# The pooling branch's product in the merge stage: one product of plain float32 tiles, or three passes over high and low parts

## The reference

```python
y_a = o @ w_branch_gla[l]
pooled = multiscale_pool(u)
y_b = jnp.einsum('blgc,gcd->blgd', pooled, w_pool_group[l]).reshape(bsz, length, D_MODEL)
y_b = (y_b * pool_scale[l]).astype(x.dtype)
merged = jax.nn.sigmoid(g_a) * y_a + jax.nn.sigmoid(g_b) * y_b
x = x + merged @ w_out[l]
```

## Time and profile before

| | us |
|---|---|
| median of 3 runs | 2587.4 (2586.15 to 2589.64) |
| profiled execution | 2586.93 |
| its span | 2585.1 |
| PE busy | 2535.0 (98%) |
| VectorE busy | 1857.0 (72%) |
| POOL busy | 1213.2 (47%) |
| ScalarE busy | 1039.5 (40%) |

### The profile page before, as it was taken

The page is one execution under the profiler, slowest core; times in us unless marked ns, Lnnn a source line. Parts: engine busy times, 40 slices in busy tenths (PEclk is TensorE's granted clock), DMA queues, the critical chain, the costliest instruction groups (busy, mean ns, idle before and its releaser), DMA issues. The chain is left out here.

```text
span 2585.1 us, 32147 instructions
## 1 busy us (share of the span) xinstructions
PE 2535.0 (98%) x12094; PEld 2051.7 (79%) x12094; DVE 1857.0 (72%) x2076; ACT 1039.5 (40%) x1463; POOL 1213.2 (47%) x764
## 2 busy tenths in 40 slices
PE   8999999999999999999999999999999999999998
PEld 6888788887787888887887778776886788878887
DVE  8756756558559666668879657666658767787988
ACT  6322444442124333234435212766455333444443
POOL 3322222224448888885333344241135888833332
PEclk9999999999999999999999999999999999999999
DMA  6433333345522343246642443402333676775544
GB/s 207 124 102 123 120 129 109 102 142 163 179 92 79 99 123 106 78 139 204 228 129 71 142 154 104 135 33 73 115 90 118 223 235 202 246 246 171 180 137 165
DMA packets 341055, 362.95 MB, mean 140 GB/s; under 512 B 21115, under 2 KB 256278, under 8 KB 340902
## 3 DMA queue, kind: packets, MB, share of 16 engines
q1 hardware_dynamic: 335686, 341.49, 41.5%
q10 hardware_dynamic: 5216, 19.40, 1.9%
HBM read 247.81 MB, written 111.99 MB: 139 GB/s over the span
## 5 line engine op out<-in xcount | busy, mean ns | idle before, releaser
L4024 PE MATMUL ps<-op_hi,sw_hi 128*128 128x512 f32 x1765 | 692.1, 392 | 10.4 <-POOL sw_lo L3920 3.1
L4024 PE MATMUL ps<-op_hi,sw_lo 128*128 128x512 f32 x1765 | 686.9, 389 | 0.0
L4024 PE MATMUL ps<-op_lo,sw_hi 128*128 128x512 f32 x1765 | 686.8, 389 | 0.0
L4024 PEld LDWEIGHTS ps<-op_hi,sw_hi 128*128 128x128 f32 x1765 | 331.3, 188 | 89.0 <-POOL sw_lo L3920 6.5
L4024 PEld LDWEIGHTS ps<-op_lo,sw_hi 128*128 128x128 f32 x1765 | 331.4, 188 | 69.4 <-issue 1.4
L4024 PEld LDWEIGHTS ps<-op_hi,sw_lo 128*128 128x128 f32 x1765 | 331.3, 188 | 69.4
L546 POOL TENSOR_TENSOR w_hi_t<-w_raw,ones 128x1024 fp32r<-128x1024 f32 (+1 forms) x54 | 99.5, 1848 | 462.6 <-DMA w_raw<-in_w_in 196.3
L3910 ACT ACTIVATE sw_hi<-sw_sumNone 128x512 fp32r<-128x512 f32 (+1 forms) x252 | 156.7, 623 | 312.8 <-PE ps L4024 205.4
L3920 POOL TENSOR_TENSOR sw_lo<-sw_sumNone,sw_hi 128x512 fp32r<-128x512 f32 x138 | 220.4, 1606 | 23.4 <-ACT sw_hi L3910 23.3
L3871 POOL TENSOR_TENSOR sw_sumNone<-sw_raw 128x512 f32<-128x512 f32 (+1 forms) x63 | 112.5, 1786 | 218.5 <-DVE sw_lo L3920 197.7
L3920 POOL TENSOR_TENSOR sw_lo<-sw_raw,sw_hi 128x512 fp32r<-128x512 f32 x109 | 156.9, 1446 | 65.4 <-ACT sw_hi L3910 65.3
(11 more groups left out here) (525 smaller groups left out, 5324.4 us busy)
## 6 DMA issues: line engine op xcount, KB each, us to landing
w_raw<-in_w_in SPq DMA_DIRECT2D x45, 512.0 KB, 4.6
sw_raw<-in_w_ffn_in SPq DMA_DIRECT2D x44, 512.0 KB, 5.4
sw_raw<-in_w_up SPq DMA_DIRECT2D x32, 512.0 KB, 7.0
hidden<-hidden_rows SPq DMA_DIRECT2D x16, 1024.0 KB, 5.0
sw_raw<-hidden SPq DMA_DIRECT2D x32, 512.0 KB, 5.4
op_raw<-down_differences SPq DMA_DIRECT2D x16, 1024.0 KB, 6.0
proj<-acc SPq DMA_DIRECT2D x56, 256.0 KB, 2.2
acc<-proj SPq DMA_DIRECT2D x28, 512.0 KB, 4.3
```

The lines of the kernel that those rows point to most:

```text
L4024: mm = pe.matmul(out, w, x[:, k, :], start=(k == 0 and i == 0 and r < 4), stop=(k == n - 1 and i == 2), skip_group_check=r >= 4)
```

## The change

The pooling branch's product is computed like the large ones. New tiles `pooled_hi`, `pooled_lo`, `wpool_hi` and `wpool_lo`, each 128x1024, hold the parts. ScalarE copies the weights into `wpool_hi` once, ahead of the first gates, and for each group the pooled rows into `pooled_hi`: the first behind gates(0), the others in rounds 1, 3 and 5 behind the gates of the next round. POOL subtracts once, `wpool_lo`, between units 1 and 2 of its sixteen. VectorE subtracts once for each group, `pooled_lo`: right behind `pool(0)`, and behind `split_lo` in rounds 1, 3 and 5. `yb(j)` is three passes of two matmuls. `pooled_ready` counts to 3 for each group instead of 1, and `wpool_loaded` to 18 instead of 16. The scan reads its ones from a column of the constant tile `ones` with step 0, where before a tile of ones was written by a memset.

```diff
--- before.py
+++ after.py
@@ -298,7 +298,7 @@
 LATER_PAIRED = {"sw_landed": ("gab_loaded", (128, 128)), "hid_stored": ("o_back", (80, 16)),
                 "x3_back": ("half_ready", (8, 8)), "x3_spilled": ("x1_spilled", (64, 64))}
 OPERANDS = (("r_loaded", 64), ("v_loaded", 64), ("qk_loaded", 128), ("o_stored", 96), ("u_loaded", 64),
-            ("gla_loaded", 128), ("wpool_loaded", 16))
+            ("gla_loaded", 128), ("wpool_loaded", 18))
 ODD_HEADS = (("merged_hi", 8), ("merged_lo", 8))
 X1_BACK = (("sc_fwd", 4), ("sc_tile", 4), ("vt_ready", 8), ("o_ready", 8))
 
@@ -1804,7 +1804,29 @@
 
         ub, csb, pooled = acc[:, 0, :], acc[:, 1:3, :].rearrange("p a t -> p (a t)"), acc[:, 3, :]
         gab = [(acc[:, 4, :], acc[:, 6, :]), (acc[:, 5, :], acc[:, 7, :])]
-        ones_row = ssq
+        ones_row = ones[:, 0:1].to_broadcast([P, T])
+        pooled_hi, pooled_lo = at("pooled_hi", [P, T], 68, F32R), at("pooled_lo", [P, T], 12, F32R)
+        wpool_hi, wpool_lo = at("wpool_hi", [P, T], 64, F32R), at("wpool_lo", [P, T], R0 + 128, F32R)
+        wpool_row = wpool[:, :, :].rearrange("p g c -> p (g c)")
+
+        def wpool_high(act):
+            act.wait_ge(S["wpool_loaded"], 16)
+            act.activation(wpool_hi[:, :], wpool_row, ACT.Copy).then_inc(S["wpool_loaded"], 1)
+
+        def wpool_low(pool):
+            pool.wait_ge(S["wpool_loaded"], 17)
+            pool.tensor_tensor(wpool_lo[:, :], wpool_row, wpool_hi[:, :].bitcast(F32), ALU.subtract)\
+                .then_inc(S["wpool_loaded"], 1)
+
+        def pooled_high(act, g):
+            act.wait_ge(S["pooled_ready"], 3 * g + 1)
+            act.activation(pooled_hi[:, :], pooled, ACT.Copy).then_inc(S["pooled_ready"], 1)
+
+        def pooled_low(dve, g):
+            dve.wait_ge(S["pooled_ready"], 3 * g + 2)
+            dve.tensor_tensor(pooled_lo[:, :], pooled, pooled_hi[:, :].bitcast(F32), ALU.subtract)\
+               .then_inc(S["pooled_ready"], 1)
+
         Z0 = 8
 
         def ya_wo_unit(sp, j):
@@ -1823,7 +1845,7 @@
                 if j:
                     sp.wait_ge(S["o_lo"], KT)
                 if j % 2 == 0 and g:
-                    sp.wait_ge(S["pooled_ready"], g)
+                    sp.wait_ge(S["pooled_ready"], 3 * g - 2)
                     sp.dma_start(ub, proj[(25 + g) * P:(26 + g) * P, :]).then_inc(S["u_loaded"], 16)
                 if j == 0:
                     sp.wait_ge(S["o_lo"], 5)
@@ -1853,18 +1875,18 @@
                         wait_k=(lambda k: pe.wait_ge(S["o_lo"], O_ORDER.index(k) + 1)) if j == 0 else None)
 
             def yb(j):
-                pe.wait_ge(S["wpool_loaded"], 16)
-                pe.wait_ge(S["pooled_ready"], j // 2 + 1)
+                pe.wait_ge(S["wpool_loaded"], 18)
+                pe.wait_ge(S["pooled_ready"], 3 * (j // 2) + 3)
                 if j == 0:
                     pe.wait_ge(S["o_rstd"], GH)
                 if j == 1:
                     pe.wait_ge(S["o_gate"], 4 * GH - 1)
                 if j >= 2:
                     pe.wait_ge(S["yb_scaled"], j - 1)
-                for b in range(2):
-                    mm = pe.matmul(yb_bank(j)[:, b * HALF:(b + 1) * HALF],
-                                   wpool[:, j // 2, j % 2 * P:(j % 2 + 1) * P],
-                                   pooled[:, b * HALF:(b + 1) * HALF], start=True, stop=True)
+                for n, (w, x) in enumerate(((wpool_hi, pooled_hi), (wpool_hi, pooled_lo), (wpool_lo, pooled_hi))):
+                    for b in range(2):
+                        mm = pe.matmul(yb_bank(j)[:, b * HALF:(b + 1) * HALF], w[:, j * P:(j + 1) * P],
+                                       x[:, b * HALF:(b + 1) * HALF], start=n == 0, stop=n == 2)
                 mm.then_inc(S["yb_ready"], 1)
 
             ya(0)
@@ -1884,10 +1906,14 @@
                 for g in gab[j % 2]:
                     act.activation(g, g, ACT.Sigmoid).then_inc(S["gates_sig"], 1)
 
+            wpool_high(act)
             gates(0)
+            pooled_high(act, 0)
             for j in range(KT):
                 if j + 1 < KT:
                     gates(j + 1)
+                if j % 2 and j < KT - 1:
+                    pooled_high(act, j // 2 + 1)
                 act.wait_ge(S["merged_ready"], j + 1)
                 act.activation(m1hi[:, j, :], stage[:, j % 2, :], ACT.Copy).then_inc(S["merged_hi"], 1)
 
@@ -1896,16 +1922,14 @@
                 low_o(dve, k)
             all_stored(dve, ALL_IN)
             dve.wait_ge(S["z_ready"], 2 * GH)
-            dve.memset(ones_row[:, :], 1.0).then_inc(S["pool_consts"], 1)
-            dve.memset(csb[:, 0:Z0 + 1], 0.0).then_inc(S["pool_consts"], 1)
-            dve.wait_ge(S["pool_consts"], 1)
+            dve.memset(csb[:, 0:Z0 + 1], 0.0).then_inc(S["pool_consts"], 2)
 
             def pool(g):
 
                 w = 2 << g
                 h = w // 2
                 dve.wait_ge(S["u_loaded"], 16 * (g + 1))
-                dve.tensor_tensor_scan(csb[:, Z0 + 1:Z0 + 1 + T], ones_row[:, :], ub, 0.0, ALU.mult, ALU.add)\
+                dve.tensor_tensor_scan(csb[:, Z0 + 1:Z0 + 1 + T], ones_row, ub, 0.0, ALU.mult, ALU.add)\
                    .then_inc(S["pool_step"], 1)
                 dve.wait_ge(S["pool_step"], 3 * g + 1)
                 dve.tensor_copy(csb[:, Z0 + 1 + T:Z0 + 8 + T], csb[:, Z0 + T:Z0 + T + 1].to_broadcast([P, 7]))\
@@ -1932,6 +1956,7 @@
                    .then_inc(S["merged_lo"], 1)
 
             pool(0)
+            pooled_low(dve, 0)
             for j in range(KT):
                 a, b = gab[j % 2]
                 u = Step(U_YA + j)
@@ -1942,6 +1967,8 @@
                     pool(j // 2 + 1)
                 if j:
                     split_lo(j - 1)
+                if j % 2 and j < KT - 1:
+                    pooled_low(dve, j // 2 + 1)
                 dve.wait_ge(S["yb_ready"], j + 1)
                 dve.wait_ge(S["gates_sig"], 2 * j + 2)
                 dve.scalar_tensor_tensor(out=b, in0=yb_bank(j)[:, :], scalar=col("pool_scale", j), in1=b,
@@ -1954,7 +1981,7 @@
 
         def wo_sp(sp):
             sp.wait_ge(S["merged_ready"], KT)
-            sp.wait_ge(S["pooled_ready"], 4)
+            sp.wait_ge(S["pooled_ready"], 12)
             sp.wait_ge(S["yb_ready"], KT)
             for j in range(2, KT):
                 ya_wo_unit(sp, KT + j)
@@ -4659,6 +4686,8 @@
             in_pool(pool)
             mid_pool(pool)
             for j in range(2 * KT):
+                if j == 2:
+                    wpool_low(pool)
                 split_unit(pool, Step(U_YA + j))
             f1_pool(pool)
             in2_pool(pool)
```

## The result

The changed kernel took 2593.34 us in the median of 20 runs (2587.17 to 2596.08), the kernel before 2589.48 in 20 runs beside it (2586.09 to 2594.72). The ratio is 1.0015, 95% interval 1.0008 to 1.0021: about 3.9 us slower (3.5 +- 1.3 in the means), inside the 0.2% that the prediction called no change, but clear of noise, against a forecast of +0.5 us. The absolute number missed by 5.4 us: 2.1 of these are the base, since the three first runs of the kernel before lay low (2587.4), and the rest is the change.

A forecast was written before the change was run, and what follows sets the result against it. TensorE bounds the kernel, busy 2535.0 of 2585.1 us. Savings of 3.2 against waits of 3.3, 0.1 and 0.4 give +0.5 us by unrounded terms, on 2587.4: 2587.9 us, range 2584.2 to 2590.3.

The forecast's parts named there:

- PE's own part: TensorE's product yb: six rounded passes at 0.2267 us, 1.36 us, saving 0.405 us each, 3.2 us over eight.
- the first wait: At yb(0), behind the pool, copy and subtraction chain: 3.3 us of stall, bounds 0.9 and 4.5 us.
- the 611.5: Sign at yb(0): the forecast is wrong if it starts before 608.5 or after 611.5 us.
- `yb(4)` without a wait: At yb(4): operands ready after 12.1 us, PE arrives after 12.24; no stall, 0.14 us to spare.
- `yb(6)` with 0.3: At yb(6): with 15 edge columns split_lo starts 0.54 us later than with 7, a stall of 0.4 us.
- the scan at 2.28 us: VectorE's scan, ones read with step 0: taken as 2.27 us; slower-scan rival +8.9 in all, chance 0.05 shared with passes.
- the weights' copy at no cost: ScalarE before the gates: copy and table load end at 593.9, gates start at 594.21; costs nothing, by 0.3 us.
- no wait at `yb(2)`: At yb(2): low half ready at 623.85, level with PE, 0.1 us; 1.0 if yb(0) waits only 0.9.
- The rival of kinder turns: VectorE and POOL before yb(0): the edge column keeps its place behind L1921; sum -0.9 us, 2586.5, chance 0.20.
- nine tenths or more in every slice: Whole kernel, premise: TensorE's granted clock is nine tenths or more in every slice of the page.
- longer stalls: Rival at two of the waits: POOL's turns fall worse, +1.8 to +4 us, up to 2591.4; chance 0.11.

The follow-up runs named there:

- e4: Kernel before, with yb as six rounded passes over existing blocks of m2hi, no copies, subtractions or waits, sums meaningless: stage 85.80 us, ratio 0.9988.
- e12: Changed kernel without POOL's subtraction; the third pass takes the high weights again, so sums are false: stage 91.40 us, ratio 1.0014.
- e2: Changed kernel with 14 useless passes on TensorE filling its idleness before yb(0), the wait kept: stage 89.77 us, ratio 1.0010.
- e1: The changed kernel run again, nothing altered: stage 92.44 us, ratio 1.0011 to the kernel before.
- e3: Changed kernel with all copies, subtractions and waits, but yb by the old plain product of two matmuls: stage 95.23 us, ratio 1.0020.
- e5: Changed kernel with POOL's wpool_low one unit later, behind unit 2: stage 91.13 us, ratio 1.0014.
- e7: Changed kernel with POOL's wpool_low one unit later, pooled_lo awaited only before yb's third pass, ScalarE's pooled_high ahead of the gates: stage 89.86 us, ratio 0.9997.
- e6: Changed kernel with yb's passes reordered and pooled_lo awaited only before the third, POOL's order unchanged: stage 89.05 us, ratio 1.0003.

## Why the prediction was wrong

**Right**: PE's own part. The new pace of 0.2267 us and the round of 12.24 us are in the profile, and e4 gives the saving by itself.

**Right**: the first wait, 3.3 us forecast and 3.4 measured, with its cause. e12 takes POOL's instruction away and the wait is gone. One turn of the chain was put in the wrong place, with no effect on its end. `yb(0)` starts at 612.05, past the 611.5 that the prediction named as a sign of being wrong, but only because `ya(1)` starts 1.66 us later in this execution than in the one before. The prediction took the turns from rows of the trace before, and L1818's 4.37 us, 2.2 of them spent waiting for VectorE's scan, show them again.

**Right**: `yb(4)` without a wait, `yb(6)` with 0.3 (forecast 0.4), the scan at 2.28 us, the weights' copy at no cost: it and the table load end at 595.50 (593.14 + 1.06, 594.22 + 1.28), and the gates start at 595.95, behind their transfer.

**Right, on thin ground**: no wait at `yb(2)`, forecast at 0.1 us. In e2, at the full clock, `yb(2)` comes 0.15 late. But the term rests on a transfer of 5.0 us read from one row, and e12 shows 6.8 and a wait of 3.4 us, where the prediction had 1.0 for an early `yb(0)`. The rival of kinder turns, at -0.9 us, was so perhaps priced too low: e12, with no first wait at all, has +2.5 by stage and `yb(7)`.

**The step that failed** is the one that was not there: "3.3 us of stall, and PE's whole queue stands behind it" priced the wait at its own length, and the clock behind it at nothing. In the profile the idleness of 3.22 us is followed by half clock, and that costs another 1.6 us (first profile) to 2.8 or 3.1 us (e1, e3). With it the stage and `yb(7)` come to +2.3 or +3.5 us where the sum had +0.5; in e2, with the same wait and the idleness filled, they come to +0.8. The totals have +3.5 +- 1.3 (+3.9 in the medians) and +3.5 +- 1.2. So most of the miss is shown in the stage; 1.2 us of the first result lie elsewhere, within its interval, and e2's totals do not show the gain of the whole clock. The trace of before would have told: it has a place with 2.1 us of idleness and a clock of 0.66 in the 5 us behind it. The page's row of the clock, in slices of 65 us, hid that, and the prediction went on from "nine tenths or more in every slice" as if no stretch were slower. The longest idleness that PE had in the stage before was 1.3 us, at 583.6, with the clock at 1.00 behind it, so the stage's own rows could not show it.

Of the rivals, "longer stalls" (+1.8 to +4) has the measured size, but not the mechanism. The range ended at 2590.3: it missed the 2593.34 by 3.0, and would have missed it by 1.0 with the base of 20 runs.

## What to carry to other kernels

Price a wait of TensorE at its length plus the half clock behind it, here 1.5 (e5) to 3.1 us (e3) for an idleness of 3.2 us, and look for idleness and the clock behind it in short stretches of the trace before, not in the slices of a page. When a new step makes two engines wait for each other's instructions, count the instructions of both in the whole stretch; moving one of them within it changed nothing here (3.22 us of idleness before `yb(0)` in the changed kernel and in e5). And when one wait is taken away, work out the next one anew from the earlier start: in e12 it grew from nothing to 3.4 us.

## What was not expected of the hardware

A 128x1 instruction of VectorE took 2.34 us because an instruction of POOL came ahead of it (e5). Idle pieces of only 0.65 and 1.36 us were followed by half clock in one kernel (e7) and not in another (e6). The same idleness of 3.22 us was followed by 3.4 us of half clock in two profiles (the changed kernel's first, e5) and by 6.8 in two others (e1, e3). And the same idleness of 2.1 us near 1655 us was followed by 0 us of it (the changed kernel's first profile) to 10.2 (e2).
